# Output norms of the full token tiles taken along the free axis, with a new order table, in a two-layer decoder trunk

## What is computed

```python
o = o * lax.rsqrt(jnp.mean(o * o, axis=-1, keepdims=True) + NORM_EPS) * gdn_norm
o = o * jax.nn.silu(z.reshape(bsz, t, GDN_HEADS, GDN_DV))
out = jnp.concatenate([o, y_sc], axis=-1) @ w_out
```

## Time and profile before

| | |
|---|---|
| three runs | 1420.73, 1414.49, 1419.95 us, median 1419.95 us |
| the profiled execution's own time | 1411.93 us |
| its span | 1410.1 us |
| PE busy | 1390.6 us (99%) |
| DVE busy | 861.4 us (61%) |
| ACT busy | 631.5 us (45%) |
| mean granted clock of PE | 0.996 |

### The profile page before, as it was taken

The page is one execution under the profiler, slowest core; times in us unless marked ns, Lnnn a source line. Parts: engine busy times, 40 slices in busy tenths (PEclk is TensorE's granted clock), DMA queues, the critical chain, the costliest instruction groups (busy, mean ns, idle before and its releaser), DMA issues.

```text
span 1410.1 us, 25253 instructions
## 1 busy us (share of the span) xinstructions
PE 1390.6 (99%) x10788; PEld 1368.2 (97%) x10788; DVE 861.4 (61%) x1510; ACT 631.5 (45%) x1002; POOL 34.2 (2%) x130
## 2 busy tenths in 40 slices
PE   9999999999999999999999999999999999999997
PEld 9999999899999999999999999998999999999997
DVE  5655533787696765553376555337977968655433
ACT  5444333582634543433344433335826355444331
POOL 0000000110000000000000000001100000000000
PEclk9999999999999999999999999999999999999998
DMA  6544344322225344334435443443221263444342
GB/s 225 206 148 150 122 144 142 131 91 72 87 75 203 120 150 140 134 128 143 163 121 195 145 150 122 144 149 125 90 97 61 91 216 121 151 149 150 124 144 99
DMA packets 49760, 190.93 MB, mean 135 GB/s; under 512 B 6160, under 2 KB 8720, under 8 KB 49136
## 3 DMA queue, kind: packets, MB, share of 16 engines
q1 hardware_dynamic: 49040, 184.19, 39.0%
q0 software_dynamic: 608, 5.12, 0.9%
HBM read 182.86 MB, written 6.43 MB: 134 GB/s over the span
## 4 chain that ended last, share of the span: by engine, by line
PE 94%; DVE 4%; ACT 1%; issue 1%; DMA 0%; SPq 0%; DVEq 0%
PE PS L1492 27%; PE PS L1493 27%; PE PS L1494 26%; PE PS L1532 2%; PE PS L1663 2%; PE PS L1537 2%; PE PS L1533 2%; PE PS L1661 1%; PE PS L1812 1%; DVE WL L1039 1%; DVE XL L1051 1%; PE PS L1704 1%; ACT XH L750 1%; PE PS L1787 1%; PE PS L1768 1%
## 5 line engine op out<-in xcount | busy, mean ns | idle before, releaser
L1492 PE MATMUL PS<-XH,WH 128*128 128x336 f32 (+1 forms) x1728 | 550.7, 319 | 0.0
L1494 PE MATMUL PS<-XH,WL 128*128 128x336 f32 (+1 forms) x1728 | 542.7, 314 | 0.0
L1493 PE MATMUL PS<-XL,WH 128*128 128x336 f32 (+1 forms) x1728 | 542.6, 314 | 0.0
L1039 DVE TENSOR_TENSOR WL<-RAW,WH 128x1024 fp32r<-128x1024 f32 (+1 forms) x312 | 398.6, 1301 | 192.1 <-ACT WH L733 191.9
L733 ACT ACTIVATE WH<-RAW 128x1024 fp32r<-128x1024 f32 (+1 forms) x312 | 343.6, 1119 | 227.9 <-DMA RAW<-in_w_down 173.8
L1492 PEld LDWEIGHTS PS<-XH,WH 128*128 128x128 f32 x1728 | 325.1, 188 | 2.2 <-DVE XL L1440 0.4
L1493 PEld LDWEIGHTS PS<-XL,WH 128*128 128x128 f32 x1728 | 325.2, 188 | 0.4
L1494 PEld LDWEIGHTS PS<-XH,WL 128*128 128x128 f32 x1728 | 324.9, 188 | 0.0
L1492 PE MATMUL PS<-HH,WH 128*128 128x336 f32 (+1 forms) x704 | 221.3, 314 | 0.0
L1493 PE MATMUL PS<-HL,WH 128*128 128x336 f32 (+1 forms) x704 | 221.3, 314 | 0.0
L1494 PE MATMUL PS<-HH,WL 128*128 128x336 f32 (+1 forms) x704 | 221.2, 314 | 0.0
(11 more groups left out here) (252 smaller groups left out, 1219.4 us busy)
## 6 DMA issues: line engine op xcount, KB each, us to landing
RAW<-in_w_up SPq DMA_DIRECT2D x176, 512.0 KB, 4.3
RAW<-in_w_down SPq DMA_DIRECT2D x64, 704.0 KB, 4.1
RAW<-in_w_in SPq DMA_DIRECT2D x56, 512.0 KB, 4.3
RAW<-in_w_out SPq DMA_DIRECT2D x16, 512.0 KB, 4.5
SEQ_S<-in_states SPq DMA_DIRECT2D x2, 2048.0 KB, 9.8
out_state_s<-SEQ_S POOLq DMA_DIRECT2D x2, 2048.0 KB, 8.9
X<-in_x SPq DMA_DIRECT2D x8, 168.0 KB, 4.4
out_y<-X SPq DMA_DIRECT2D x4, 320.0 KB, 2.3
```

Source lines behind the costliest of these rows:

```text
L1039: dve.tensor_tensor(WL[slot][:, cols], RAW[slot][:, cols], WH[slot][:, cols].bitcast(F32), ALU.subtract).then_inc(split_lo.sem, 1)
L1492: pe.matmul(out, wh, xh, start=first, stop=False)
L1493: pe.matmul(out, wh, xl, start=False, stop=False)
L1494: return pe.matmul(out, wl, xh, start=False, stop=last)
```

## The change

In the full tiles (t = 0, 1) the two products of `o` swap their operands, so that the output has tokens on partitions. The sum of squares becomes a DVE reduction along the free axis (`reduce_sum`), and the four products of `o_cols` are gone from PE. The reciprocal root is then a scale per partition: a new step `o_scale` multiplies the output by it on ACT, one activation a head. `rob` transposes the scaled output on PE instead of spreading the root, and DVE multiplies what is in PSUM by gain and gate in one operation instead of two. Tile 2 stays as it was. `HEAD` and `BEHIND_PART` are replaced throughout; a line of them is shown.

```diff
 HEAD = [
-    ("entry",), ("gate_rows",), ("gate_read",), ("evac", 0), ("hi", 1, 0), ("evac", 1), ("tap", 0), ("tap", 1), ("gate_cols",),
-    ("hi", 1, 1),
+    ("entry",), ("gate_rows",), ("evac", 0), ("evac", 1), ("tap", 0), ("gate_read",), ("hi", 1, 0), ("hi", 1, 1), ("evac", 2),
 ]
...
                     elif what == "o_cols":
                         act.wait_ge(to_act.sem, to_act.at(3 + NTH[step], layer))
                         act.activation(T1[:, t, :], T0[:, t, :], ACT.Sqrt).then_inc(to_dve.sem, 1)
+                    elif what == "o_scale":
+                        act.wait_ge(o_inv.sem, o_inv.at(NTH["o_inv", t], layer))
+                        own = kT(tcols(t))
+                        for h in range(HEADS):
+                            ins = act.activation(own[:, h, :], own[:, h, :], ACT.Copy, scale=RO[:, t, h:h + 1])
+                        ins.then_inc(o_scaled.sem, 1)
...
                     elif what == "o_cols":
-                        dve.wait_ge(small.sem, small.at(1 + NTH[step], layer))
-                        dve.scalar_tensor_tensor(T0[:, t, :], O_COLS[:, t, :], 1.0 / P, WQ[:, t, :],
+                        if t == C_TILE:
+                            dve.wait_ge(small.sem, small.at(1, layer))
+                            sums = O_COLS
+                        else:
+                            act_group(("o", t), layer)
+                            sums = T2[:, t, :]
+                            ch.step(dve.reduce_sum(sums, vT(tcols(t)), AXIS.X))
+                        dve.scalar_tensor_tensor(T0[:, t, :], sums, 1.0 / P, WQ[:, t, :],
                                                  ALU.mult, ALU.add).then_inc(to_act.sem, 1)
...
                         rob = group(step, layer)
+                        if t != C_TILE:
+                            dve.wait_ge(act_out.sem, silu_of("z", HEADS - 1, layer))
+                            evacuated(dve.scalar_tensor_tensor(kT(cols), rob, PAR_ALL[:, layer, C_GN:C_GN + 1], ZS[:, :, cols],
+                                                               ALU.mult, ALU.mult))
+                            continue
...
                         for h in range(HEADS):
-                            pe.matmul(out[:, h, :], NVP[:, t, h, :], QKM[:, t, h, :], start=True, stop=False)
-                            ins = pe.matmul(out[:, h, :], PR_S[:, h, :], qT(tcols(t))[:, h, :], start=False, stop=True)
+                            pe.matmul(out[:, h, :], QKM[:, t, h, :], NVP[:, t, h, :], start=True, stop=False)
+                            ins = pe.matmul(out[:, h, :], qT(tcols(t))[:, h, :], PR_S[:, h, :], start=False, stop=True)
...
-                            pe.wait_ge(o_inv.sem, o_inv.at(NTH["o_inv", t], layer))
-                            per_head_products(step, layer, lambda h: RO[:, t, h:h + 1].to_broadcast([P, P]), None, transpose=True)
+                        if t == C_TILE:
+                            pe.wait_ge(o_inv.sem, o_inv.at(NTH["o_inv", t], layer))
+                            per_head_products(step, layer, lambda h: RO[:, t, h:h + 1].to_broadcast([P, P]), None, transpose=True)
+                        else:
+                            pe.wait_ge(o_scaled.sem, o_scaled.at(NTH["o_scale", t], layer))
+                            per_head_products(step, layer, lambda h: kT(tcols(t))[:, h, :], None, transpose=True)
```

More of the change, by code:

```diff
@@ L21 @@
 ACT = mybir.ActivationFunctionType
+AXIS = mybir.AxisListType
 P = 128
@@ L171 @@
-    [("val_lo", 0), ("oC",), ("place", 1), ("hi", 10, 0), ("val_twin", 0), ("yt", 0, 64), ("key_lo", 1), ("conv", 17), ("o", 2),
-     ("y", 1, 32), ("vt", 0), ("val_hi", 1)],
-    [("evac", 19), ("key_twin", 1), ("spread", 0, 0)],
-    [("sn", 0, 0), ("ks", 0)],
-    [("spread", 1, 0), ("lo", 10, 0), ("vt", 1), ("evac", 20), ("nv", 0), ("val_lo", 1), ("o_cols", 2), ("spread", 2, 0), ("x", 1, 64),
-     ("o_inv", 2), ("tap", 19), ("sn", 1, 0)],
-    [("o", 0), ("spread", 3, 0), ("hi", 10, 1), ("rob", 2), ("evac", 21), ("st", 0), ("lo", 10, 1), ("val_twin", 1), ("o_cols", 0)],
@@ L188 @@
[L188 to L196 removed]
+    [("gate_cols",), ("lo", 1, 0), ("conv", 0), ("tap", 1)],
+    [],
@@ new lines @@
+    [],
+    [("qk", 0), ("unit", 2)],
+    [("nt", 2), ("kk", 0)],
+    [("evac", 11), ("qk", 1), ("unit", 0), ("read", 0), ("lo", 5, 0), ("tap", 10)],
+    [("x", 2, 2), ("kk", 1)],
+    [("unit", 1), ("y", 2, 2)],
+    [("hi", 5, 1), ("silu", 9), ("nt", 0), ("hi", 6, 0), ("nt", 1), ("evac", 12)],
+    [("x", 0, 2), ("x", 2, 4), ("y", 0, 2), ("x", 1, 2), ("x", 0, 4)],
+    [("mirror", 2, 2), ("read", 1), ("mirror", 0, 2), ("y", 1, 2), ("lo", 5, 1), ("y", 0, 4), ("conv", 10), ("mirror", 1, 2),
+     ("hi", 6, 1), ("lo", 6, 0)],
@@ new lines @@
+    [("silu", 15), ("lo", 7, 0), ("key_hi", 0), ("mirror", 0, 16)],
+    [],
+    [("key_norms",)],
+    [("hi", 8, 0), ("place", 0), ("read", 6), ("evac", 16)],
+    [],
+    [],
+    [("evac", 17), ("lo", 7, 1), ("hi", 8, 1), ("y", 0, 32), ("lo", 8, 0), ("hi", 9, 0), ("y", 1, 8), ("mirror", 1, 8), ("lo", 8, 1),
+     ("vt", 2), ("read", 7)],
+    [("vt", 0), ("evac", 18), ("x", 1, 16)],
+    [("kst",)],
+    [("key_hi", 1), ("nv", 2), ("x", 0, 64)],
+    [],
+    [("val_hi", 0), ("val_hi", 1), ("key_lo", 0), ("y", 1, 16), ("key_twin", 0), ("st", 2), ("conv", 17)],
@@ new lines @@
+    [("oC",), ("o", 2), ("lo", 9, 0), ("hi", 9, 1), ("mirror", 1, 16), ("evac", 19), ("val_lo", 0), ("x", 1, 32), ("yt", 0, 64),
+     ("val_lo", 1), ("ks", 0), ("conv", 19), ("tap", 17), ("lo", 9, 1), ("val_twin", 0), ("key_lo", 1), ("evac", 20), ("spread", 0, 0),
+     ("spread", 1, 0)],
+    [("place", 1), ("kt", 0), ("hi", 10, 0)],
+    [("nv", 0), ("o_cols", 2), ("y", 1, 32), ("o_inv", 2), ("hi", 10, 1), ("sn", 0, 0), ("spread", 2, 0), ("val_twin", 1)],
+    [("x", 1, 64), ("lo", 10, 0), ("kt", 1), ("o", 0), ("sn", 1, 0), ("st", 0), ("evac", 21), ("o_cols", 0), ("yt", 1, 64),
+     ("sn", 2, 0)],
@@ new lines @@
+    [("key_twin", 1), ("vt", 1), ("tap", 19), ("spread", 3, 0), ("o_inv", 0), ("rob", 2), ("o_scale", 0), ("hi", 11, 0)],
+    [("sn", 3, 0), ("o_low", 2), ("tap", 21)],
+    [("ks", 1), ("hi", 11, 1)],
+    [("lo", 10, 1), ("nv", 1), ("conv", 21), ("spread", 0, 1), ("evac", 22), ("rob", 0)],
+    [],
+    [("sn", 0, 1), ("o", 1), ("o_low", 0), ("spread", 1, 1), ("evac", 23)],
+    [("o_cols", 1)],
+    [],
+    [("hi", 12, 0), ("lo", 11, 0), ("o_inv", 1), ("lo", 11, 1), ("evac", 24)],
+    [("spread", 2, 1), ("sn", 1, 1)],
@@ new lines @@
+    [("lo", 12, 0), ("hi", 12, 1), ("tap", 23)],
+    [("evac", 25), ("o_scale", 1), ("rob", 1), ("sn", 2, 1)],
+    [("o_low", 1), ("hi", 13, 0), ("conv", 23), ("spread", 3, 1)],
+    [("lo", 12, 1)],
+    [("st", 1)],
+    [("evac", 26), ("tap", 25), ("lo", 13, 0)],
+    [],
+    [("hi", 13, 1), ("evac", 27), ("conv", 25), ("sn", 3, 1), ("finish",), ("out_o", 0), ("out_o", 1), ("out_o", 2), ("out", 0),
+     ("out", 1), ("out_o", 3), ("out", 2), ("out", 3), ("out", 4), ("out", 5), ("out", 6), ("out", 7)],
```

108 lines of the change are left out of this document (35 added, 73 removed), and 6 rows, old and new, of the table BEHIND_PART.

## The result

The changed kernel takes 1422.02 us in the median of 13 executions (1415.9 to 1430.88), the kernel before 1414.49 us in 13 (1410.92 to 1420.73). The ratio is 1.0048, 95% interval 1.0025 to 1.0071. The change makes the kernel slower by about half a per cent. The time is inside the range that was given; the forecast was a change of -0.1%, so the sign is not the one that was forecast.

The account below looks back on a forecast made before the run. PE, busy 99% of the span, was taken as the bound. Terms -3.2 - 1.2 - 2.0 + 4.4 + 0.8 = -1.2 us (-0.1%) gave 1410.7 on the profiled execution, 1418.5 as median; likeliest case 1415 to 1422, chance 0.50.

Parts of the forecast that it names:

- one-column products: Four `o_cols` products a full tile leave PE, 0.81 us each group; two tiles in two layers give -3.2 us.
- gate rows: `gate_cols` moves from the head to behind part 4,0; its wait of 0.7 us a layer goes, -1.2 us in all.
- crossings: Switches on PE between projection products and small tiles: 10 fewer a layer at about 0.1 us, -2.0 us for both.
- waits: New PE waits at the end, at `nv 2`, in inversion groups and for bank reuse: 2.2 us a layer, +4.4 for both.
- stalls of issue: PE stopping for missing instructions among dense small groups, slot 14,0: +0.8 us for both layers, between -2.4 and +9.
- clock: Rival: PE's fall to its lower clock, seen once at 292.6, goes or comes again; -3 or +2 us, chance 0.05.
- Instructions run short: Rival: dense groups in slots 14,0 and 15,2 to 16,0 outrun instruction supply; +3.8 us, or 1424 to 1426 total; chance 0.16.
- the waits at `nv 2`: PE waits for DVE's VS between `kst` and `nv 2`, 0.4 us a layer.
- those at `out 0`: PE waits for XL at the end because the last `sn` reading stands between the last convolutions; 0.7 us a layer.
- the inversion: PE waits between dependent y and x groups, twice in slot 14,0, once in 16,0, some in 15,2; 0.9 us a layer.
- it costs nothing on PE: Between `o 0` and `rob 0`, over 7 us of PE work covers the DVE and ACT chain of about 4 us.
- The rival in which the one-column products are worth little: Removing the 16 products gives 0.8 us in place of 3.2, so 1421 us in total; chance 0.07.

Follow-up runs that it names:

- shift32_timed: Changed kernel with 32 more PE records (tiny products) ahead of layer 0's mixer, timed in twelve executions: 1412.63 us, ratio 0.9988.
- shift32_late1: Changed kernel with 32 more PE records ahead of layer 0's mixer and, in layer 1 only, two weight bursts one tile later: 1408.06 us, ratio 0.9945.
- pause: Kernel before with one PE pause of about 3.2 us a layer, at a quiet place behind tile 7's last product: 1427.6 us, ratio 1.0086.
- combo: Changed kernel with slot 14,0's groups spread, two weight loads a layer one tile later, last `sn` back ahead of `evac 26`: 1418.88 us, ratio 1.0019.

## Why the prediction was wrong

Its single terms, against what the profiles show (both layers, us):

| term | predicted | measured |
|---|---|---|
| one-column products | -3.2 | -3.2 or a little more: their group fell from 5.8 us busy (48 records, in the profile before) to 1.9 (16) |
| gate rows | -1.2 | -1.3, the wait is gone |
| crossings | -2.0 | about -2.2, as the rest |
| waits | +4.4 | about +5.4: XL 1.5, VS 0.8, SQX 0.6 more, `sn` 0.9, inversion about 1.6 more |
| stalls of issue | +0.8 | +3.3 |
| clock | 0 | +4.9 |

The inversion's waits don't stand in the view of waits, but the distances from start to start show them. In the lines of `shift32_timed` above, the five groups of slot 14,0 take 1.96 us from the first start to the return to the projection; four distances of 0.27 and the 0.37 from a group's start to the return make 1.45. So PE waits 0.5 us there, where the prediction had twice 0.24. Counted in the same way over all groups of levels 2 to 16, `shift32_late1` has 1.1 and 1.0 us in its two layers and before 0.2 and 0.4. The crossings are a remainder. From the mixer's first product that waits for XH to `out 0`, before takes 176.03 us in layer 0 (258.24 to 434.27) and 172.86 in layer 1 (962.93 to 1135.79), `shift32_late1` 172.56 (258.70 to 431.26) and 172.08 (959.95 to 1132.03). Less stalls and slow stretches that is 173.16 and 171.66 against 172.56 and 170.98. So the change gives 1.3 us clear of these. The one-column products, the gate rows and the waits sum to +0.9, which leaves -2.2 for the crossings. In the changed kernel's own profile (258.93 to 438.76 and 967.43 to 1142.81) the same subtraction gives 2.0 in place of 1.3, so the remainder is good to about 1 us.

The groups of the changed kernel by shape, one-column products and the reduction (busy us, mean ns):

```profile
L1896 PE MATMUL PS<-MK,QKV 128*128 128x1 f32 x16 | 1.9, 240 | 0.0
...
L1429 DVE TENSOR_REDUCE TOK<-QKV 128x4 f32<-128x512 f32 x4 | 2.7, 680 | 0.0
```

**The step that failed** is "The stalls of issue": "between -2.4 (none left) and +9 (the rival below) I take +0.8 for both layers". It measured +3.3, and the clock behind it +4.9. Two things were wrong in it. First, I took a rate, 260 records in 3.8 us, where there are borders: 3.6 to 3.8 us a block without weights on the way and up to 6.3 with them. The same five groups cost 3.1 us or nothing, by 32 instructions that stand some 75 us earlier. I had the block size in the earlier trace rows and did not count to its borders. Second, I gave no price to the burst of weights, which starts with slot 14,0; it held this block up by 1.1 us.

**The clock** was a rival of its own at 0.05, with "-3 or +2 in all". `pause` shows that it can follow idle time, so it belonged to the price of a long stall. Here the rival "Instructions run short" (0.16) was right in place and mechanism, with 3.1 us in slot 14,0 where it said 2.8, and 2.2 us in slot 16,0, in one layer, where it said 1.3 in both. What it lacked was the clock behind, 4.9 us, where it had added 2 to 3 us for a block that comes late. Its sign, "issue" of more than 2 us at one place in slots 14 to 16, came true.

**Luck.** The time lies in the range, but not by the sum, which had -1.2 us where +7.5 was measured. The three runs that the forecast was set on have a median 5.5 us above that of the 13 executions of before, and this took up most of the difference.

**Right**: the value of the one-column products; the reduction, 0.68 us where 0.69 was taken, so that DVE's total did not change; the ACCX wait; the waits at `nv 2`, 0.36 and 0.41 for 0.4; those at `out 0`, 0.73 and 0.74 for 0.7; the inversion, 0.8 us a layer more for 0.9, though the sentence that the tightest places before show no wait was wrong, since the earlier trace rows has one of 0.16; and, as far as a remainder tells, the crossings. The wait at `out 0` was right in size only: it was said to come from the moved reading, and `combo` moved it back without effect. **Not seen**: the waits of 0.2 to 0.3 for SQX and of 0.4 to 0.5 at a product of `sn`, which the timeline puts behind DVE's SB, named "issue". The 0.2 a layer for a bank in slots 20,2 to 22,0 didn't come. PE's busy time did not fall by 3 to 6 us as a sign of being right, since the clock took it back; in `shift32_late1` it is 6.6 below before. And "it costs nothing on PE" for the new chain through DVE and ACT holds on the new table alone; on the old one it cost 3.4 us.

The rival in which the one-column products are worth little falls: 16 fewer of them took 3.9 us off their group's busy time.

## What to carry to other kernels

Where small products stand densely, count instructions, not only time: find the borders at which PE stops, and see whether each block of 256 lasts longer than its fetch and whether a burst of weights starts just ahead of the request. Before judging a new order by half a per cent, run it at another place of the borders; a few dummy instructions are enough, and they moved one and the same order from 1422 to 1412.6 us. Price a stall of PE of 2 us or more with the slower clock behind it, which cost 1.7 to 6.8 us a stretch here, and compare the mean granted clock over the executions beside the medians.

## What the runs showed of the hardware

- PE's instructions come in blocks of 256, and every stall of issue in the table stands at a border; a block arrives 3.6 to 3.8 us after the last border was passed (3.4 to 4.4 over all profiles, with one of 2.4), 4.3 to 6.3 us with 0.5 to 1.05 MB of weights on the way, and it can be asked for earlier where PE comes to the border slowly (1.4 us ahead in `shift32`).
- The packet starts 2.3 to 2.7 us before PE goes on, in all of them.
- A wait of 3.2 us at a place away from the inversion's groups brought the granted clock to 0.50 for 6.8 us in one layer and 3.4 in the other; the whole cost of two such waits was 13.3 us in the median.
- The clock was also at 0.50 for 3.4 to 6.8 us where PE had not stood still for more than 0.3 us just ahead (`before` at 292.6, `combo` at 993.3). What lowers it there, and in executions whose stalls are short, stays open.
